# The conditioning products of a three-block transformer: from split fp32r pairs to plain fp32 in four column groups

## What is computed

```python
c_act, cc_act = silu(c), silu(c_ctx)              # (1, 2048) and (2048,)
for i in range(2):                                # retention, attention
    mod_l = c_act  @ ada_w[i] + ada_b[i]          # ada_w: (2, 2048, 6144)
    mod_c = cc_act @ ada_w[i] + ada_b[i]
    shift, scale, gate = split(mod, 3)            # for each of the two
    h = rms_norm(x, gain[i]) * (1 + scale) + shift
    ...                                           # mixer, heads of it
    x = x + gate * y
```

## Time and profile before

| | |
|---|---|
| median of 3 runs | 3681.36 us (3678.01 to 3681.5) |
| the profiled execution | 3680.96 us, its span 3679.6 us |
| PE matmul busy | 3426.3 us (93%) |
| PE weight loads busy | 2957.6 us (80%), beside the matmuls |
| DVE busy | 1973.0 us (54%) |
| ACT busy | 1448.0 us (39%) |
| mean DMA rate | 138 GB/s |

### The profile page before, as it was taken

How to read it: one execution, slowest core, us unless ns; L and a number is a source line. 1 busy time by engine, 2 the same in 40 slices (tenths; PEclk the granted TensorE clock), 3 DMA queues, 4 the chain that set the end, 5 groups by cost and what they waited for, 6 DMA issues and landing times.

```text
span 3679.6 us, 48681 instructions
## 1 busy us (share of the span) xinstructions
PE 3426.3 (93%) x20506; PEld 2957.6 (80%) x20506; DVE 1973.0 (54%) x2701; ACT 1448.0 (39%) x1976; POOL 0.2 (0%) x4
## 2 busy tenths in 40 slices
PE   5989999999999999999988999997999899999998
PEld 3867788787878778787866778886999899999998
DVE  7665443444443343444447576766666555555555
ACT  5555322323232322323234645444554434444443
POOL 0000000000000000000000000000000000000000
PEclk7999999999999999999999999998999999999999
DMA  8765332323223232323235433443545444455554
GB/s 305 235 234 173 104 103 92 115 92 109 97 98 103 82 124 92 110 96 109 92 111 171 138 103 126 132 132 101 172 149 166 137 142 167 149 187 184 184 178 144
DMA packets 140777, 509.32 MB, mean 138 GB/s; under 512 B 15248, under 2 KB 19472, under 8 KB 140048
## 3 DMA queue, kind: packets, MB, share of 16 engines
q1 hardware_dynamic: 137040, 493.03, 40.5%
q10 hardware_dynamic: 3520, 13.17, 0.9%
HBM read 501.95 MB, written 4.19 MB: 138 GB/s over the span
## 4 chain that ended last, share of the span: by engine, by line
PE 78%; DVE 10%; ACT 5%; DMA 4%; issue 3%; ACTq 0%; SPq 0%; DVEq 0%
PE bank L437 24%; PE bank L438 24%; PE bank L439 24%; DVE w_lo L1261 4%; DMA raw<-stream 4%; ACT w_hi L817 2%; PE bank L568 1%; PE bank L623 1%; DVE a_rstd L1551 1%; PE bank L642 1%; PE bank L570 1%; PE bank L553 1%; ACT a_s L1017 1%; DVE a_numbers L1580 1%; DVE a_s L1574 0%
## 5 line engine op out<-in xcount | busy, mean ns | idle before, releaser
L1261 DVE TENSOR_TENSOR w_lo<-raw,w_hi 128x1024 fp32r<-128x1024 f32 x936 | 1130.2, 1223 | 799.3 <-ACT w_hi L817 793.4
L817 ACT ACTIVATE w_hi<-raw 128x1024 fp32r<-128x1024 f32 x936 | 971.1, 1055 | 1094.8 <-PE bank L439 988.0
L437 PE MATMUL bank<-h_hi,w_hi 128*128 128x256 f32 (+1 forms) x4160 | 1314.6, 316 | 16.0 <-DVE w_lo L1261 10.3
L438 PE MATMUL bank<-h_lo,w_hi 128*128 128x256 f32 (+1 forms) x4160 | 1296.8, 312 | 0.0
L439 PE MATMUL bank<-h_hi,w_lo 128*128 128x256 f32 (+1 forms) x4160 | 1296.8, 312 | 0.0
L437 PEld LDWEIGHTS bank<-h_hi,w_hi 128*128 128x128 f32 x4160 | 796.6, 191 | 64.9 <-DVE w_lo L1261 11.1
L438 PEld LDWEIGHTS bank<-h_lo,w_hi 128*128 128x128 f32 x4160 | 796.6, 191 | 47.5 <-issue 4.3
L439 PEld LDWEIGHTS bank<-h_hi,w_lo 128*128 128x128 f32 x4160 | 796.1, 191 | 42.7
L487 PE MATMUL bank<-w_hi,cond_parts 128*4 128x256 f32 x768 | 204.2, 300 | 73.2 <-DVE w_lo L1261 71.7
L437 PE MATMUL bank<-w_hi,h_hi 128*128 128x512 f32 x640 | 260.1, 406 | 9.1 <-DVE h_lo L1675 4.4
L438 PE MATMUL bank<-w_lo,h_hi 128*128 128x512 f32 x640 | 257.0, 402 | 0.0
(11 more groups left out here) (223 smaller groups left out, 2940.0 us busy)
## 6 DMA issues: line engine op xcount, KB each, us to landing
raw<-stream SPq DMA_DIRECT2D x936, 512.0 KB, 3.5
res<-tokens_in ACTq DMA_DIRECT2D x1, 4096.0 KB, 14.8
vg<-mem_in ACTq DMA_DIRECT2D x1, 2048.0 KB, 10.5
res<-mem_kv ACTq DMA_DIRECT2D x2, 1024.0 KB, 9.3
out<-res SPq DMA_DIRECT2D x4, 512.0 KB, 3.0
mem_kv<-qk ACTq DMA_DIRECT2D x1, 1024.0 KB, 7.8
mem_kv<-vg ACTq DMA_DIRECT2D x1, 1024.0 KB, 11.1
tab<-tables ACTq DMA_DIRECT2D x1, 577.0 KB, 4.4
```

Source lines behind the costliest of these rows:

```text
L437: pe.matmul(out, sh, mh, start=start, stop=False)
L438: pe.matmul(out, sh, ml, start=False, stop=False)
L817: act.activation(m.w_hi[n % SLOTS][:, :], m.raw[n % SLOTS][:, :], ACT.Copy).then_inc(s.hi, 1)
L1261: dve.tensor_tensor(m.w_lo[slot][:, :], m.raw[slot][:, :], m.w_hi[slot][:, :].bitcast(F32), ALU.subtract).then_inc(s.lo, 1)
```

## The change

Modulation chunks are no longer split. PE multiplies them as plain fp32 straight from `raw`. The condition vectors become a stationary block of 32 columns (`cond`, 2 used, 30 zero), and the four k tiles of a chunk go to four groups of 32 columns of the array: their outputs are partitions 0 to 31, 32 to 63, 64 to 95 and 96 to 127 of one bank. A block is now 16 matmuls. `part` is 128 x 256, and the turn sums over all 128 partitions.

`raw` is now freed for a modulation chunk by PE (`s.mm`), for any other by DVE (`s.lo`) as before. `SPLIT` lists the 744 chunks that are still split, `Q[c]` counts those before chunk c; the split buffers are taken in that count. A chunk is still split at most three past the call's own.

Small things go with it: three tables of ones are set in place and not scaled from a loaded one, a mask of the attention layer is bf16, two waits on DVE's own earlier writes are added, and a few buffers are moved.

```diff
+RAW_USE = [b[0][0] == "ada" for b in STREAM]
+SPLIT = [c for c in range(CHUNKS) if not RAW_USE[c]]
+Q = [0]
+for _raw in RAW_USE:
+    Q.append(Q[-1] + (not _raw))
...
-        self.cond_parts = sb("cond_parts", [P, KT, 4], F32R)
-        self.part = [sb(f"part{i}", [4, L]) for i in range(2)]
+        self.cond = sb("cond", [P, KT, 32])
+        self.part = [sb(f"part{i}", [P, L]) for i in range(2)]
...
-        self.mask1 = sb("a_mask", [P, 2, T])
+        self.mask1 = sb("a_mask", [P, 2, T], BF16)
...
-        if c >= SLOTS:
-            sp.wait_ge(s.lo, c - SLOTS + 1)
+        if c >= SLOTS and RAW_USE[c - SLOTS]:
+            sp.wait_ge(s.mm, c - SLOTS + 1)
+        elif c >= SLOTS:
+            sp.wait_ge(s.lo, Q[c - SLOTS] + 1)
         sp.dma_start(m.raw[slot][:, :], d["stream"][c]).then_inc(s.raw[slot], 16)
...
-        pe.wait_ge(s.lo, c + 1)
-        return m.w_hi[c % SLOTS], m.w_lo[c % SLOTS]
+        pe.wait_ge(s.lo, Q[c] + 1)
+        return m.w_hi[Q[c] % SLOTS], m.w_lo[Q[c] % SLOTS]
...
-        out = bank("ada", layer, n)[0:4, 0:L]
+        out = bank("ada", layer, n)[:, 0:L]
         for c in range(4):
-            wh, wl = weights(FIRST["ada", layer, n] + c)
-            for k in range(4):
-                kk, w = 4 * c + k, slice(k * L, (k + 1) * L)
-                pe.matmul(out, m.cond_parts[:, kk, :], wh[:, w], start=kk == 0, stop=False)
-                mm = pe.matmul(out, m.cond_parts[:, kk, :], wl[:, w], start=False, stop=kk == KT - 1)
+            chunk = FIRST["ada", layer, n] + c
+            pe.wait_ge(s.raw[chunk % SLOTS], 16 * (chunk // SLOTS + 1))
+            for j in range(4):
+                mm = pe.matmul(out[32 * j:32 * j + 32, :], m.cond[:, 4 * c + j, :],
+                               m.raw[chunk % SLOTS][:, j * L:(j + 1) * L], start=c == 0, stop=c == 3)
             mm.then_inc(s.mm, 1)
...
-            mm = pe.matmul(out[:, 2 * j:2 * j + 2], m.part[n % 2][0:4, j * P:(j + 1) * P], ones_parts[0:4, :],
+            mm = pe.matmul(out[:, 2 * j:2 * j + 2], m.part[n % 2][:, j * P:(j + 1) * P], ones_parts,
...
-    def weights_before(c):
-
-        while split[0] < min(c, CHUNKS):
-            n = split[0]
+    def weights_to(c):
+
+        while split[0] < min(Q[c] + SLOTS, len(SPLIT)) and SPLIT[split[0]] < c + SLOTS:
+            n, raw = split[0], SPLIT[split[0]]
             split[0] += 1
-            act.wait_ge(s.raw[n % SLOTS], 16 * (n // SLOTS + 1))
+            act.wait_ge(s.raw[raw % SLOTS], 16 * (raw // SLOTS + 1))
             if n >= SLOTS:
-                act.wait_ge(s.mm, n - SLOTS + 1)
-            act.activation(m.w_hi[n % SLOTS][:, :], m.raw[n % SLOTS][:, :], ACT.Copy).then_inc(s.hi, 1)
+                act.wait_ge(s.mm, SPLIT[n - SLOTS] + 1)
+            act.activation(m.w_hi[n % SLOTS][:, :], m.raw[raw % SLOTS][:, :], ACT.Copy).then_inc(s.hi, 1)
 
     def ahead(what, n=2):
 
-        weights_before(FIRST[what] + n - 1 + SLOTS)
+        weights_to(FIRST[what] + n - 1)
...
-    act.wait_ge(*s["dve_step"].at("cond"))
-    act.activation(m.cond_parts[:, :, 0:2], m.cond[:, :, :], ACT.Copy).then_inc(*s["cond_act"].up("hi"))
-    weights_before(SLOTS)
+    weights_to(0)
     act.dma_start(m.mem_raw, d["mem_in"]).then_inc(s.load["mem_in"], 16)
...
+        if c >= 2:
+            dve.wait_ge(*s["h_lo"].at(layer, 2 * c - 3))
         for k in (2 * c, 2 * c + 1):
...
```

More of the change, by code:

```diff
@@ L58 @@
 DIFF0 = 384
-TABLES, TABLES_N = columns([("diff", 896), ("ident", P), ("ones", P), ("sum_parts", 2)])
+TABLES, TABLES_N = columns([("diff", 896), ("ident", P), ("sum_parts", 2)])
 MASK2_N = 2 * L + 2 * N_DIL * L
@@ L328, in __init__ @@
         self.half_gain = sb("half_gain", [P, RET_V // P])
+        self.lg = sb("lg", [P, 2 * RET_HEADS])
+        self.nlg = sb("nlg", [P, 2 * RET_HEADS])
         self.cond_t = sb("cond_t", [P, KT, 2])
-        self.cond = sb("cond", [P, KT, 2])
         self.lt = [sb(f"lt{i}", [P, 2 * RET_HEADS]) for i in range(4)]
@@ L845, in ada_part @@
             act.wait_ge(*s["ada_turned"].at(layer, n - 2))
-        act.activation(m.part[n % 2][:, :], psum("ada", layer, n)[0:4, 0:L], ACT.Copy).then_inc(*banks.up("ada", layer, n))
+        act.activation(m.part[n % 2][:, :], psum("ada", layer, n)[:, 0:L], ACT.Copy).then_inc(*banks.up("ada", layer, n))
     def root(what, meaned, out):
@@ L1227, in scalar_program @@
     for p in range(KT // 2):
-        weights_before(FIRST["pb", p] + SLOTS)
+        weights_to(FIRST["pb", p])
         for j in range(2):
@@ L1231, in scalar_program @@
         for j in range(2):
-            weights_before(FIRST["pa", p, j] + SLOTS)
+            weights_to(FIRST["pa", p, j])
             gate(p, "ga", j, (p, "gb", j))
-            weights_before(FIRST["pm", p, j] + SLOTS)
+            weights_to(FIRST["pm", p, j])
             gate(p, "gm", j, (p, "ga", j))
@@ L1260, in weights_before @@
             slot = n % SLOTS
-            dve.tensor_tensor(m.w_lo[slot][:, :], m.raw[slot][:, :], m.w_hi[slot][:, :].bitcast(F32), ALU.subtract
+            dve.tensor_tensor(m.w_lo[slot][:, :], m.raw[raw % SLOTS][:, :], m.w_hi[slot][:, :].bitcast(F32), ALU.subtract
                               ).then_inc(s.lo, 1)
     def ahead(what, n=2):
-        weights_before(FIRST[what] + n - 1 + SLOTS)
+        weights_to(FIRST[what] + n - 1)
     def done(what, n=2):
@@ L1335, in vector_program @@
     dve.memset(m.eps[:, :], EPS).then_inc(*step.up("eps"))
+    dve.memset(m.cond[:, :, :], 0.0).then_inc(*step.up("zero"))
     cond_in = m.param("cond").rearrange("p (k b) -> p k b", b=2)
     dve.wait_ge(s.load["par"], 16)
+    dve.wait_ge(*step.at("zero"))
     dve.wait_ge(*s["cond_act"].at("tanh"))
-    dve.scalar_tensor_tensor(out=m.cond[:, :, :], in0=m.cond_t[:, :, :], scalar=1.0, in1=cond_in, op0=ALU.add,
+    dve.scalar_tensor_tensor(out=m.cond_t[:, :, :], in0=m.cond_t[:, :, :], scalar=1.0, in1=cond_in, op0=ALU.add,
                              op1=ALU.mult).then_inc(*step.up())
     dve.wait_ge(*step.now())
-    dve.tensor_scalar(m.cond[:, :, :], m.cond[:, :, :], 0.5, None, ALU.mult).then_inc(*step.up("cond"))
-    dve.wait_ge(*s["cond_act"].at("hi"))
-    dve.tensor_tensor(m.cond_parts[:, :, 2:4], m.cond[:, :, :], m.cond_parts[:, :, 0:2].bitcast(F32), ALU.subtract
-                      ).then_inc(*s["cond_done"].up())
-    weights_before(SLOTS)
+    dve.tensor_scalar(m.cond[:, :, 0:2], m.cond_t[:, :, :], 0.5, None, ALU.mult).then_inc(*s["cond_done"].up())
+    weights_to(0)
     logit = m.param("logit")
@@ L1394, in vector_program @@
         ks = range(4 * (n - 4), 4 * (n - 4) + 4)
+        if n > 4:
+            dve.wait_ge(*s["h_lo"].at("mem", ks[0] - 1))
         for k in ks:
@@ L1430, in vector_program @@
         else:
-            weights_before(FIRST["v", 0] + c + 24 + SLOTS)
+            weights_to(FIRST["v", 0] + c + 24)
     ada_add(0, 23)
@@ L1523, in vector_program @@
     dve.wait_ge(*s["rstd"].at("x1"))
-    dve.tensor_scalar(m.ones_head[:, :], m.table("ones"), 1.0 / HEAD, None, ALU.mult).then_inc(*s["added"].up("ret", RET_HEADS - 1))
+    dve.memset(m.ones_head[:, :], 1.0 / HEAD).then_inc(*s["added"].up("ret", RET_HEADS - 1))
     dve.tensor_scalar(m.gains[:, 0:1], m.param("q_gain"), HEAD ** -0.5, None, ALU.mult)
```

31 lines of the change are left out of this document (13 added, 18 removed).

## The result

The changed kernel takes 3709.26 us (median of 4 runs, 3705.82 to 3712.88), the kernel before beside it 3681.43 us (3678.01 to 3682.16): a ratio of 1.0078, interval 1.006 to 1.0095. It is slower, by 0.8%, and 25 us above the forecast of 3684, inside the range.

A forecast was written before the change was run, and what follows sets the result against it. The modulation was taken as bound by its supply, DVE and the loads, and only then by PE; gains and losses summed to +3 us on the profiled 3680.96, forecast 3684 us, range 3640 to 3755.

The forecast's parts named there:

- Projections, the wait: Memory projections: block to next tile takes 10.2 us, before 5.5 in the mean, in seven rounds: +33 us.
- The clock there: Memory projections: after PE's longer idle, the first 3 us of a tile run at half clock, seven times: +10 us.
- the chosen case: PE in modulation blocks: column groups overlap two-fold, 3.4 us a block or 0.85 us a chunk; chance 0.34.
- The bursts: Loads in a row: the first lands after 3.4 us, the next after 2.3, each further one after 1.27.
- The start: Start of the kernel, 90 us before: 76 us after the change, -15 us (-22 to -5).
- head 7: Five blocks around head 7: 36 us in place of 45.1, -9 us.
- the end: Five blocks at the end of the layer: 32 us in place of 43.5, -12 us.
- the way from block 15 to the first value chunk: First values, ahead of value chunk 0: 15.4 us in place of 22.3, and 1 more from a shorter block: -8 us.
- Value rounds: First values, six rounds of 12.1 us: later loads +2 us, lower clock after PE's idle +6 (0 to 9).
- Heads 0 to 6: Pair of blocks to first value chunk: 15.1 us in place of 15.9, -6 us over seven heads; lower clock +2.
- The rest: After 2039.8 us, where no modulation is left: 1640 us stay, predicted 0.
- The rival of full overlap: PE in modulation blocks: four column groups run side by side, 0.43 us a chunk, 3672 us in all; chance 0.22.

The follow-up runs named there:

- e13_after_six_then_four: The changed kernel with six raw slots and three buffers for split halves up to the last modulation chunk, then four and four: 3614.96 us.
- e10_six_raw: The changed kernel with six raw slots in place of four and three buffers for split halves in place of four throughout: 3649.71 us.

## Why the prediction was nearly right, and where its steps failed

The mechanism held: PE's and DVE's savings are real, and they are eaten by loads that start late, in the projections above all. The measured terms, against those of the sum:

- **Projections, the wait: +31, predicted +33.** From block to tile 10.1, 9.2, 10.2, 9.9, 10.5, 10.1 and 9.7 us, where 10.2 was worked out and 5.5 is the mean of before. The parts agree too: ACT took the third chunk 7.75 us after the block's start, 8.25 predicted.
- **The clock there: +15, predicted +10.** From a tile's start to the next block it is 13.6 to 14.1 us in the eight rounds; before, it was 11.6 in six of them and 12.9 and 13.1 in the first and the last. I had charged the first 3 us of a tile, from the earlier trace rows; the granted clock of 0.84 over 14.01 us in the window above means 4.5 us at the lower level.
- **The overlap: the chosen case was wrong.** I took two-fold from the pairs of records, 3.4 us a block; it is 1.93, and 7.09 without overlap, so all four groups run side by side. The pairs show how the program's matmul is recorded, and nothing of how long a group of columns is taken. The Trainium skill, "TensorE: Matmul & The Clock Gate", Part 3, says that column tiles run concurrently, and the trace agrees with it: the four start 6 to 7 ns apart, where the page has some 4. It should have been the case for PE. The same part says that a weight load overlaps a matmul only when the row group differs; here 32 loads of 32 columns are busy for 1.45 us within the block's 1.93, all over the same rows, so the measurement decides against the rule as it stands.
- **The bursts: the rest of the miss.** I gave each chunk of a burst 1.27 us, the step at which ACT took chunks at the start of before. That was with eight chunks of room. With four slots, each waits for PE and then for its load, and the measured rates are 345, 300 and 317 GB/s in the start, head 7 and the end, or 1.5 to 1.75 us a chunk. The start gave 9.5 us and not 15, head 7 6.6 and not 9, the end 6.8 and not 12, and the way from block 15 to the first value chunk 3.3 and not 8: 18 us less than the sum had. With six slots the start moves 395 GB/s, 1.33 us a chunk, and is 8 us shorter, so in the start the number of slots limited the rate, and not the loads alone.
- **Value rounds: +9.9, predicted +2 and +6.** Six rounds of 13.7 us in place of 12.1. **Heads 0 to 6: -3, predicted -4**: from pair to value chunk 15.4 us in the mean of the seven, 15.8 before; 14.7 in head 0, 15.2 before. **The rest: -1.1, predicted 0.**

These add up to the 22 us between the forecast's +3 and the +25 measured: 18 from the bursts, 5 from the clock, 2 from the rounds and 1 from the heads, less 2 from the wait, 1 from the rest and 1 elsewhere. The rival of full overlap, which described PE rightly, gave 3672 and would have been 37 us off, because it carried the same bursts. So the forecast was nearer by luck: its error in the overlap, 12 us on the slow side, offset a part of its error in the bursts. Between the chances, 0.42 for slower was the highest, but with 0.38 for faster beside it the prediction hardly told the sign; its bursts should have been priced by what four slots can carry.

PE's own saving of 96 us, which the prediction worked out for full overlap, is 48 x (3.8 - 1.93) = 91 us by the two traces. The nearness to the 94 us between the changed kernel and e13_after_six_then_four means nothing: these are counted from the changed kernel and with two more raw slots, and against the kernel before the gain is 67.

Left open: what the remaining 3 us of idle in a round of e10_six_raw would give, since no run has more than six slots; what six raw slots or the spread order would give to the kernel before; and what decides, behind idles of the same length, whether the clock falls.

## What to carry to other kernels

A change that lets the last engine of a pipeline read straight from the load buffer takes away the stage in between and its buffers: count the chunks that can lie ahead before and after, and price each burst by slots over a slot's whole cycle, not by the fastest step in the trace. What an earlier stage no longer does was worth little here until its memory went back into prefetch: six raw slots and a spread order made of a loss of 28 us a gain of 150. The better order of "copy the result" and "prepare what is next" on a helper engine turned here with the supply: copying first gained 45 us where the loads came late and cost 57 where the chunks lay ready.

## What the runs showed of the hardware

- Four plain fp32 matmuls of 256 columns in four groups of 32 columns take 0.48 us (1.93 / 4), one alone 0.44 (7.09 / 16); their weight loads, 1.45 us in a block, lie within the 1.93.
- Idles of 3.0 to 3.3 us in rounds of 20 us left all the tiles of 96 matmuls behind them at 13.9 to 14.2 us in e10_six_raw, where 11.6 is the time at the full clock; idles of 6.1 to 7.4 us left them at 13.7 to 14.1 in the changed kernel. Behind 3.1 us the first such tile of e13_after_six_then_four took 11.7. With 6.2 us of unused matmuls in the idle, six of seven took 11.7.
- The 8.48 us wait at 53.19 in the start of the changed kernel falls into the 4 MB load of the tokens, 15.5 us from issue to landing. The four chunks issued beside it took 13.1 us in the median to land, where the median of all is 3.8; the engines moved 404 GB/s in that wait.
